# Twelve small loads of each layer leave GpSimd's queue for ScalarE's and SyncE's

## The reference

```python
sh1, sc1, g1, sh2, sc2, g2 = modulation(c, w_ada, b_ada)      # silu(c) @ w_ada, 1024 x 6144
h = rms_norm(x, norm1_g) * (1 + sc1) + sh1
qa, ka, va, qb, kb, vb, cq, ckv, kr = split_projection(h @ w_in)   # 1024 x 1824
# three kinds of attention (windowed with a sink, neighbourhood with a bias, latent),
# for the latent tokens also over a cached context of 128 tokens
x = x + g1 * (concat(oa, ob, oc) @ w_out)
x = x + g2 * moe_ffn(rms_norm(x, norm2_g) * (1 + sc2) + sh2)   # 64 experts, top 6, and a shared one
```

## Time and profile before

| | us |
|---|---|
| median of 3 runs | 1288.08 |
| the three runs | 1286.6, 1288.08, 1289.69 |
| profiled execution, its own time | 1287.52 |
| its span in the trace | 1285.6 |
| PE busy | 1214.6 (94%) |
| PE clock granted, mean over the span | 0.982 |
| moved by DMA | 494.99 MB, 385 GB/s |

### The profile page before, as it was taken

One profiled execution on the slowest core, in us unless ns is written; L12 is line 12 of the kernel. 1 busy time (PEld: TensorE's weight loads), 2 busy tenths in 40 slices (PEclk: granted clock), 3 DMA queues, 4 the chain that ended last, 5 costly groups with the idle time before them and its releaser, 6 DMA issues.

```text
span 1285.6 us, 22837 instructions
## 1 busy us (share of the span) xinstructions
PE 1214.6 (94%) x9511; PEld 800.7 (62%) x9511; DVE 310.9 (24%) x883; ACT 192.9 (15%) x471; POOL 52.1 (4%) x97
## 2 busy tenths in 40 slices
PE   8989999998999999987999999999999999999795
PEld 4435776665667667654544568666557776676463
DVE  2037452123111111110130664321311111111012
ACT  1016221010111111010020351111011011110011
POOL 1330011000000000000020100000000000000000
PEclk9989999999999999998989999999999999999899
DMA  9988989999999999999995895989999999999995
GB/s 365 398 332 355 403 340 360 372 418 421 420 421 420 421 419 422 419 421 420 410 373 199 342 364 198 388 339 420 420 421 420 420 420 420 421 421 421 420 420 198
DMA packets 82117, 494.99 MB, mean 385 GB/s; under 512 B 8908, under 2 KB 13472, under 8 KB 28512
## 3 DMA queue, kind: packets, MB, share of 16 engines
q1 hardware_dynamic: 77984, 484.73, 92.4%
q0 software_dynamic: 3488, 8.29, 2.0%
q10 hardware_dynamic: 544, 0.52, 0.1%
HBM read 491.20 MB, written 2.50 MB: 384 GB/s over the span
## 4 chain that ended last, share of the span: by engine, by line
PE 57%; issue 25%; DMA 8%; DVE 4%; SPq 3%; POOL 1%; ACT 1%; POOLq 0%; ACTq 0%; DVEq 0%
PE ps L1363 14%; PE ps L1306 8%; PE ps L1396 7%; PE ps L1328 6%; PE ps L908 5%; DMA ring<-in_exp_w_down 5%; PE ps L1136 4%; PE ps L875 3%; PE ps L1259 2%; DMA spare<-in_exp_w_up 2%; SPq L603 2%; DMA ring<-in_w_ada 1%; PE ps L1093 1%; SPq L598 1%; PE ps L1118 1%
## 5 line engine op out<-in xcount | busy, mean ns | idle before, releaser
L1363 PE MATMUL ps<-ring,kt_buf 128*32 128x256 f32 (+2 forms) x3008 | 285.0, 384 | 18.3 <-DMA spare<-in_exp_w_up 13.4
L1363 PEld LDWEIGHTS ps<-ring,kt_buf 128*32 128x32 f32 (+2 forms) x3008 | 169.7, 120 | 106.5 <-issue 38.0
L1306 PE MATMUL ps<-kt_buf,attn 128*128 128x128 f32 x1472 | 184.6, 279 | 1.8 <-DVE kt_buf L1994 1.8
L1306 PEld LDWEIGHTS ps<-kt_buf,attn 128*128 128x128 f32 x1472 | 173.7, 193 | 16.9 <-issue 14.3
L1328 PE MATMUL ps<-kt_buf 128*128 128x256 f32 x704 | 163.8, 385 | 3.2 <-DVE kt_buf L2112 1.8
L1396 PE MATMUL ps<-ring,kt_buf 128*32 128x512 f32 (+2 forms) x768 | 158.4, 613 | 8.5 <-DMA ring<-in_exp_w_down 8.5
L1328 PEld LDWEIGHTS ps<-kt_buf 128*128 128x128 f32 x704 | 130.3, 190 | 55.9 <-issue 22.4
L1363 PE MATMUL ps<-spare,kt_buf 128*32 128x256 f32 (+1 forms) x608 | 106.7, 391 | 0.0
L908 PE MATMUL ps<-ring,ht 128*128 128x456 f32 x256 | 99.2, 548 | 0.3 <-DVE ht L1670 0.3
L2100 DVE SCALAR_TENSOR_TENSOR kt_buf<-kt_buf,ps 128x256 f32<-128x256 f32 x44 | 18.5, 421 | 323.1 <-ACT kt_buf L1595 323.1
L1396 PEld LDWEIGHTS ps<-ring,kt_buf 128*32 128x32 f32 (+2 forms) x768 | 42.0, 123 | 67.4 <-issue 64.1
(11 more groups left out here) (313 smaller groups left out, 1108.0 us busy)
## 6 DMA issues: line engine op xcount, KB each, us to landing
ring<-in_exp_w_gate SPq DMA_DIRECT2D x104, 1024.0 KB, 19.5
ring<-in_exp_w_down SPq DMA_DIRECT2D x92, 1024.0 KB, 22.0
ring<-in_exp_w_up SPq DMA_DIRECT2D x84, 1024.0 KB, 19.1
ring<-in_w_ada SPq DMA_DIRECT2D x10, 3072.0 KB, 11.8
spare<-in_exp_w_up SPq DMA_DIRECT2D x22, 1024.0 KB, 26.3
spare<-in_exp_w_gate SPq DMA_DIRECT2D x16, 1024.0 KB, 10.8
attn_w<-in_exp_w_up SPq DMA_DIRECT2D x12, 1024.0 KB, 24.5
ring<-in_w_ada SPq DMA_DIRECT2D x5, 2048.0 KB, 10.6
```

Of the source, the lines that this page charges most:

```text
L1306: last = pe.matmul(ps[:, 4 + b, (c % 4) * P:(c % 4 + 1) * P], h2[:, t, c * P:(c + 1) * P], pick[:, t, :], start=(t == 0), stop=(t == NG - 1))
L1363: last = pe.matmul(ps[w * e:w * (e + 1), b, 0:DE], xg[:, k, w * e:w * (e + 1)], half_of(chunk_of(l, load_of(part, i, e)))[:, k, :], start= ...
```

## The change

The twelve loads become one function, `small_loads(eng, l)`, which takes the issuing engine. Layer one's are issued by ScalarE, behind its wait for the third half product (`half_mm` 3) and ahead of its two loads of constants. Layer two's are issued by SyncE, behind the fourth entry of that layer's ring, `("in", 2)`, and behind waits for the last readers of the two expert chunks that lie in `attn` and `attn_w`. The bias rows of layer two move, on GpSimd, from layer one's gate to the opening of layer two. The wait for `s_small` stands where it stood, and so does the order on PE and VectorE.

```diff
+        def small_loads(eng, l):
+            for dst, src in ((w_uq, I["c_w_uq"][l].rearrange("(k p) n -> p k n", p=P)),
+                             (w_ukv, I["c_w_ukv"][l]),
+                             (cache_ak, I["cache_a_k"][0, l].rearrange("t h d -> t (h d)")),
...
+                             (cache_kr, I["cache_c_krope"][0, l]),
+                             (w_router[:], I["router_w"][l].rearrange("(k p) n -> p k n", p=P)),
+                             (rbias[:], I["router_bias"][l:l + 1, :].to_broadcast([P, E])),
+                             (kvg[:], I["c_kv_norm_g"][l:l + 1, :].to_broadcast([P, CKV])),
+                             (sink[:, 0:8].rearrange("p (j a) -> p j a", j=2)[:, :, 0:A_GROUP],
...
+                eng.dma_start(dst, src).then_inc(s_small, 16)
...
@@ SyncE, in the loop over entries[l] @@
+                    if l and i == NSLOT - 1:
+                        for c in (ATTN_C, ATTN_W_C):
+                            part_b, step_b, _ = LOADS[LAST[c]]
+                            sp.wait_ge(S[used_by[part_b]], done - (STEPS - 1 - step_b))
+                            settle()
+                        small_loads(sp, l)
@@ GpSimd @@
                     pool.wait_ge(S["half_mm"], 4)
                     pool.wait_ge(s_skew, 16)
-                    bias_table(0)
-                    small_loads(0)
-
-                attention_loads(l)
+                bias_table(l)
                 pool.wait_ge(s_skew, 16 + 16 * 12 * (l + 1))
...
-                if l + 1 < DEPTH:
-                    pool.wait_ge(S["key"], l + 1)
-                    small_loads(l + 1)
-                    bias_table(l + 1)
@@ ScalarE @@
+            act.wait_ge(s_set, 6)
             act.wait_ge(S["half_mm"], 3)
+            small_loads(act, 0)
             act.dma_start(tbl[:, 0:C_ID], consts[:, 0:C_ID]).then_inc(s_const, 16)
             act.dma_start(tbl[:, C_ID + P:], consts[:, C_ID + P:]).then_inc(s_const, 16)
```

More of the change, by code:

```diff
@@ L518, in copy_set @@
                 eng.tensor_scalar(dst, src, scale, None, ALU.mult).then_inc(S["qk_d"], 1)
+        def small_loads(eng, l):
+            for dst, src in ((w_uq, I["c_w_uq"][l].rearrange("(k p) n -> p k n", p=P)),
+                             (w_ukv, I["c_w_ukv"][l]),
+                             (cache_ak, I["cache_a_k"][0, l].rearrange("t h d -> t (h d)")),
+                             (cache_av, I["cache_a_v"][0, l].rearrange("t h d -> t (h d)")),
+                             (cache_bk, I["cache_b_k"][0, l].rearrange("t h d -> t (h d)")),
+                             (cache_bv, I["cache_b_v"][0, l].rearrange("t h d -> t (h d)")),
+                             (cache_ckv, I["cache_c_kv"][0, l]),
+                             (cache_kr, I["cache_c_krope"][0, l]),
[3 more added lines that the diff above has]
+                             (sink[:, 0:8].rearrange("p (j a) -> p j a", j=2)[:, :, 0:A_GROUP],
+                              I["a_sink"][l:l + 1, :].rearrange("o (j a) -> o j a", j=2)
+                              .to_broadcast([P, 2, A_GROUP]))):
+                eng.dma_start(dst, src).then_inc(s_small, 16)
         @block.sync
@@ L548, in settle @@
                 sp.sem_inc(s_sp, 1)
+            used_by = {"gate": "gl", "up": "gu", "down": "y1"}
             done = 0
@@ L605, in load_half @@
                                  ).then_inc(there, 16)
-                used_by = {"gate": "gl", "up": "gu", "down": "y1"}
                 def attention_done():
@@ L706, in _ @@
         def _(pool):
[L707 to L725, removed]
             def bias_table(l):
```

## The result

The changed kernel takes 1302.7 us in the median of 4 runs (1298.95 to 1304.18), the kernel before 1288.24 (4 runs, 1286.6 to 1289.69). The ratio is 1.0111, 95% interval 1.0092 to 1.013: slower. The profiled execution is the fastest of the four: 1298.95 us with a span of 1297.1, 11.5 above the span of before.

A forecast was written before the change was run, and what follows sets the result against it. PE was taken to set the pace up to layer one's gate, the weight stream behind it. Span 1285.6 + 21.1 + 2.4 - 7.4 = 1301.7, so 1304 us; range 1286 to 1311, likeliest case 1297 to 1311.

The forecast's parts named there:

- Part one: Layer one, between projection and w_uq product: PE's wait for the small loads goes, 6.97 us instead of 14.34, -7.4 us.
- Part two: Layer one's projection: ScalarE's held issues delay `ht_a`, so PE waits from 50.8 to 71.9 us, +21.1 us.
- The clock: Behind PE's new wait in layer one the granted clock is low once more: +2.4 us, bounds 1.7 and 3.4.
- Part three: GpSimd in layer one loses 12 issues and its bias loads come earlier; nothing waits: 0.
- Part four: Layer two's opening: SyncE is held until 678 us at the latest, `("in", 3)` and small loads still in time: 0.
- Part five: Layer one's gate loses 16 DMAs that slowed the weight stream, which has idle time anyway: 0, at most -0.6 us.
- The sum: Whole kernel: 1285.6 + 21.1 + 2.4 - 7.4 = 1301.7 us of span, with the shift ahead of the gate going through to the end.
- Not held: Rival: ScalarE's queue takes all loads or drains short packets faster, `ht_a` at 50.3 or 52.5, 1280 or 1282 us; chance 0.16.
- gain and loss cancel: Rival: a deeper ScalarE queue puts `ht_a` between 54 and 59 us, 1286 to 1290 us; chance 0.04.
- SyncE is held too: Rival: ScalarE's waiting issue also blocks SyncE's load of 51.04, `ht_a` at 63, +7.3 us, 1295 us; chance 0.12.

The follow-up runs named there:

- e4: The changed kernel, but ScalarE issues layer one's twelve small loads behind the instructions that make `ht_a`: 1280.65 us, ratio 0.9949 to the kernel before.
- e2: The change in layer one alone; layer two's loads and bias rows stay with GpSimd as in the kernel before: 1301.84 us, ratio 1.011.
- e3: The changed kernel, but SyncE's first w_ada ring load, and those behind it, wait until `ht_a` is there: 1283.16 us, ratio 0.9971.
- e8: The changed kernel, but SyncE issues layer one's twelve small loads behind the opening's loads, ScalarE only its constants: 1277.43 us, ratio 0.9923.
- e9: The changed kernel, but only the first six of layer one's small loads stand ahead of ScalarE's constants, six behind `ht_a`: 1278.72 us, ratio 0.9928.
- e5: The changed kernel, but GpSimd issues layer one's router load of 1024 packets behind its bias rows: 1297.55 us, ratio 1.0074.
- e7: The changed kernel, but layer one's router load is read in 128 runs of 2 KB instead of 1024 of 256 bytes: 1298.98 us, ratio 1.0083.
- e1: The change in layer two alone; in layer one GpSimd issues all twelve loads behind the bias rows: 1287.33 us, ratio 1.0 to the kernel before.
- e6: The kernel with layer one's loads on ScalarE behind `ht_a`, but layer two's loads and bias rows as before the change: 1281.72 us, ratio 0.9947.

## Why the prediction was right, point by point

The prediction was 1304 us, slower; measured was 1302.7.

- **Part one, the wait removed, -7.4: right.** From the projection's end to the w_uq product the changed kernel takes 6.77 us (99.08 to 105.85), expected were 6.97. e4, in which this is the only part that acts, gained 6.8 us in the median (4.8 to 8.4 by its interval).
- **Part two, ScalarE held, +21.1: right in size (21.44), and shown.** e2 has the whole loss, e3 takes away the turn-taking and with it three quarters of the hold, e4, e8 and e9 take the held issues away from before `ht_a` and the wait is gone. But one of its inputs was wrong. I took from SyncE's queue that an issue is let in with 1140 to 1340 ahead; on ScalarE's it was 1010 to 1089, and 1414 behind the router. That the sum came out is because SyncE's queue is all but empty near 65 us whatever the depth (the load issued at 50.93, and 14.5 us to land as in the earlier trace rows), and q10 then moves 600 packets per us, not the 345 that I had from packets of 1 KB. So the time did not test the depth, and that a wrong depth did no harm is luck. The depth that I then took for e5 and e7, 1450 as at the changed kernel's rbias, did matter and failed: it gave waits of 5 to 8 and 8 to 11 us, and they were 16.76 and 16.26.
- **The clock, +2.4: 2.1** in the profiled execution, inside its bounds.
- **Part three, GpSimd, 0: right.** Its rows and loads are waited for nowhere: DVE goes through L1806, where the bias is wanted, at 101.20 without a wait.
- **Part four, layer two, 0: right, and shown by e1** (1.0, 0.9991 to 1.0009). I had SyncE held until 678 at the latest for an opening at 651, which is up to 27 us; measured were 21.6. The hold was not one long issue, as I had it, but six of 1.66 to 4.91 us, and the first of them is already the fourth load.
- **Part five, the gate, 0 to -0.6: not contradicted.** e6 and e4 agree, but 0.6 us is less than their intervals can tell.
- **The sum.** At the gate the shift is +16.1 as worked out (21.1 + 2.4 - 7.4 = 16.1). In the profiled execution 3.9 of it come back between the two gates and 0.7 behind, in that of e2 1.4 of 16.7 in all. In the median of the timed runs the loss is 14.5 us. What the sum has a little too large is that all of the shift goes through to the end; what gives some of it back was not tested.

The rivals. *Not held* and *gain and loss cancel* are refuted by ScalarE's timeline, with `ht_a` at 72.14. *SyncE is held too* is refuted by one row: SyncE's issue at 50.93 took 0.38 us in the middle of ScalarE's hold of 16.45. By the lock that the Trainium skill tells of ("Perfetto Trace Analysis", section "DMA Instruction — HWDGE (DVE, Sync)") that issue would have had to wait; a sequencer that waits for room in its queue does not, as this row shows, keep another one out. The rule of whole packets of 9 to 17 descriptors (the Trainium skill, "DMA: Bandwidth & Descriptors", section "Queues, rings and completion order") disagrees with this trace again: 38, 39 and 40 records, then 93 and 94. Nor do ScalarE's packets come in bursts: from 47 to 54 us every quarter of a microsecond has 7 to 12 of them.

## What to carry to other kernels

Before a load is moved to a compute engine's queue, count the runs of all loads that will be outstanding on that queue, not their bytes. Here an issue with up to about 1024 of them ahead cost 0.45 us (1.4 us at most); beyond that the engine stood still until the queue had drained, at about 41 packets per us, because each short packet took turns with one of 8 KB. Then ask what stands behind the issue on that engine. In this kernel the same loads gained 0.5 to 0.8% behind the one result that PE was waiting for, or on an engine that would only have waited, and cost 1.1% ahead of it.

## What the runs showed that I had not expected

- An issue on ScalarE's queue is let in with 1010 to 1089 packets ahead of it (once 1193) when the load before it is small, but with 1404 to 1693 behind the router's load of 1024, near the moment when SyncE's queue runs empty.
- A queue all but alone moved 600 packets per us, most of 256 bytes (66 to 68 us, 798 of them in the second of the two), where packets of 1 KB went at 345.
- Removing 1024 (e5) or 896 (e7) of 2944 packets shortened the wait only from 21.4 to 16.8 and 16.3 us: most of what was taken away would have moved at 600 per us once SyncE's queue was empty, and the packets that must move in turns with that queue set the length of the wait.
